# A two-layer decoder trunk on one core: router logits reordered around the last token tiles, a shorter token table, fewer identity products

## What is computed

```python
x = x + g_m * y                      # residual after the mixer's output product
h = modulate(rms_norm(x, norm_ffn[i]), sh_f, sc_f)
# hier_moe(h):
g_prob = softmax(t @ w_group);  g_idx = argmax(g_prob + b_group)
e_logit = (t @ w_router)[..group g_idx..];  e_prob = softmax(e_logit)
_, e_idx = top_k(e_prob + b_router[g_idx], 2)      # two experts of 32 for each token
out[token] += weight * (silu(t @ w1[e]) * (t @ w3[e])) @ w2[e]
```

## Time and profile before

| | us |
|---|---|
| median of 3 runs | 1144.45 |
| lowest and highest | 1142.14, 1145.19 |
| the profiled execution | 1145.37 |
| its span in the trace | 1143.6 |

### The profile page before, as it was taken

How to read it: one execution, slowest core, us unless ns; L and a number is a source line. 1 busy time by engine, 2 the same in 40 slices (tenths; PEclk the granted TensorE clock), 3 DMA queues, 4 the chain that set the end, 5 groups by cost and what they waited for, 6 DMA issues and landing times.

```text
span 1143.6 us, 15372 instructions
## 1 busy us (share of the span) xinstructions
PE 1049.5 (92%) x5698; PEld 637.9 (56%) x5698; DVE 608.2 (53%) x1464; ACT 328.1 (29%) x894; POOL 91.9 (8%) x129
## 2 busy tenths in 40 slices
PE   4999999999998999897889999999999999978997
PEld 3444444655466666564556566655457765655663
DVE  6899988897646322221256577767235622212224
ACT  4321122874231111111124545666112112111110
POOL 1000000000011111111000000000000111101110
PEclk9999999999998999999999999999998999999999
DMA  9929868918468999999996200301826799999999
GB/s 368 402 76 404 330 255 336 421 56 354 167 269 350 401 418 418 418 418 419 416 386 265 111 1 28 146 13 38 337 94 267 298 412 421 419 411 406 419 416 360
DMA packets 66816, 341.45 MB, mean 299 GB/s; under 512 B 11111, under 2 KB 11367, under 8 KB 36401
## 3 DMA queue, kind: packets, MB, share of 16 engines
q1 hardware_dynamic: 49952, 297.68, 64.5%
q0 software_dynamic: 15120, 37.63, 8.5%
q10 hardware_dynamic: 1664, 5.09, 1.1%
HBM read 320.90 MB, written 37.24 MB: 313 GB/s over the span
## 4 chain that ended last, share of the span: by engine, by line
PE 79%; DMA 7%; DVE 5%; issue 3%; ACT 3%; SPq 2%; DVEq 0%; ACTq 0%; POOLq 0%
PE PP L888 18%; PE PP L681 12%; PE PP L796 10%; PE PP L903 9%; PE PP L703 3%; DMA AHS<-in_moe_w 3%; PE PP L1111 3%; PE PP L1071 3%; PE PP L654 2%; PE PP L861 2%; PE PP L1115 2%; PE PP L740 2%; PE PP L751 2%; PE PP L690 2%; SPq L518 2%
## 5 line engine op out<-in xcount | busy, mean ns | idle before, releaser
L681 PE MATMUL PP<-ring,AHS 128*128 128x512 f32 x320 | 139.9, 592 | 0.0
L1982 DVE TENSOR_TENSOR PS<-PS,PP 128x256 f32<-128x256 f32 x33 | 13.9, 421 | 195.7 <-PE PP L888 186.1
L796 PE MATMUL PP<-ring,AHS 128*128 128x512 f32 x256 | 111.3, 593 | 1.4 <-ACT AHS L1444 0.8
L1989 DVE SCALAR_TENSOR_TENSOR PS<-PP,small,GF 128x512 f32<-128x512 f32 x66 | 46.5, 746 | 110.2 <-PE PP L903 100.3
L681 PEld LDWEIGHTS PP<-ring,AHS 128*128 128x128 f32 x320 | 59.7, 190 | 69.8 <-issue 69.8
L888 PE MATMUL PP<-RQK,RV 128*64 128x256 f32 x640 | 75.4, 392 | 10.1 <-issue 8.0
L796 PEld LDWEIGHTS PP<-ring,AHS 128*128 128x128 f32 x256 | 48.1, 190 | 59.7 <-issue 59.7
L888 PE MATMUL PP<-ring,RV 128*64 128x256 f32 (+1 forms) x608 | 75.6, 389 | 6.2 <-issue 3.2
L1502 ACT ACTIVATE PS<-PP 128x256 f32<-128x256 f32 x33 | 12.7, 384 | 216.6 <-PE PP L888 216.6
L888 PEld LDWEIGHTS PP<-RQK,RV 128*64 128x64 f32 x640 | 56.1, 142 | 32.0 <-issue 18.6
L888 PE MATMUL PP<-AHS,RV 128*64 128x256 f32 x640 | 71.7, 379 | 0.3 <-issue 0.3
(11 more groups left out here) (348 smaller groups left out, 1677.7 us busy)
## 6 DMA issues: line engine op xcount, KB each, us to landing
AHS<-in_moe_w SPq DMA_DIRECT2D x61, 1024.0 KB, 22.6
ring<-in_moe_w SPq DMA_DIRECT2D x58, 1024.0 KB, 19.6
RQK<-in_moe_w SPq DMA_DIRECT2D x52, 1024.0 KB, 20.2
ring<-in_ada_t SPq DMA_DIRECT2D x22, 1024.0 KB, 8.4
AHS<-in_ada_t SPq DMA_DIRECT2D x18, 1024.0 KB, 7.5
X<-in_moe_w SPq DMA_DIRECT2D x16, 1024.0 KB, 22.3
ring<-in_da_w_qkv SPq DMA_DIRECT2D x10, 1024.0 KB, 11.1
RQK<-in_ada_t SPq DMA_DIRECT2D x8, 1024.0 KB, 6.6
```

What stands on the lines that cost most here:

```text
L681: last = mm(PB[qkv_bank(n)][:, :], HT[:, c, t * P:(t + 1) * P], us[c // 4][:, (c % 4) * NH:(c % 4 + 1) * NH], start=c == 0, stop=c == C - 1)
L796: last = mm(PB[2 * t + n][:, :], (OT, OTM)[l][:, k, t * P:(t + 1) * P], us[k // 2][:, (k % 2) * D + n * NH:(k % 2) * D + (n + 1) * NH], st ...
L1989: last = stt(ysb[b][:, cols], PB[5 + m][:, :], weight, GF[:, cols], ALU.mult, ALU.mult)
```

## The change

1. In `project_out`, the seven identity products are gone and the logits of tile 2 stand in their place, ahead of turning tile 3. Tile 2 adds its chunks in the order 4 to 7, 0 to 3; tile 3 in the order 0, 1, 4, 5, 2, 3, 6, 7.
2. `logits` waits before every second chunk for the engine that writes it, no longer for the whole tile from both engines. For the fourth tile in the norms k = 1 and 3 each engine signals twice, after its first two chunks and after its last two. Two helper functions compute the counts.
3. `norm` on ScalarE modulates chunk 0 of tile 2 ahead of the squares of tile 3, and chunks 1 to 3 behind them. `norm` on VectorE modulates tile 2 ahead of normalising tile 3.
4. `token_v` holds S - token for both experts, and `idx` is written by one instruction in the place of three.
5. The last `keep_busy` in `route` has 16 products in layer 1, and still 22 in layer 0.

The places it touches, as a diff:

```diff
+def by_scalar(k, t, half=1):
+    last = k % 2 and t == T - 1
+    return 4 * k + k // 2 + t + 1 + (half if last else 0)
+
+def by_vector(k, t, half=1):
+    return by_scalar(k, t, half) - T
 ...
                 def logits(t):
-                    modulated(k1, t)
-                    for c in range(C):
+                    order = {2: (4, 5, 6, 7, 0, 1, 2, 3), 3: (0, 1, 4, 5, 2, 3, 6, 7)}.get(t, range(C))
+                    for n, c in enumerate(order):
+                        if c % 2 == 0:
+                            name, count = (("hA", by_scalar), ("hD", by_vector))[c // 4]
+                            pe.wait_ge(sem(name), count(k1, t, c // 2 % 2))
 ...
                 transpose_x(k1, 2)
                 logits(1)
-                keep_busy(3, 7)
+                logits(2)
                 transpose_x(k1, 3)
-                logits(2)
                 logits(3)
 ...
-                keep_busy(3, 22)
+                keep_busy(3, 16 if l else 22)
 ...
             def norm(k):                                   # ScalarE
                 squares(k, 0)
-                for t in range(T):
-                    if t + 1 < T:
-                        squares(k, t + 1)
-                    modulate(k, t)
+                squares(k, 1)
+                modulate(k, 0)
+                squares(k, 2)
+                modulate(k, 1)
+                modulate(k, 2, (0,))
+                squares(k, 3)
+                modulate(k, 2, (1, 2, 3))
+                modulate(k, 3)
 ...
             def norm(k, update):                           # VectorE
                 for t in range(T):
                     update((k - 1) // 2, t)
+                    if t == T - 1:
+                        modulate(k, t - 1)
                     normalise_x(k, t)
-                    if t:
+                    if 0 < t < T - 1:
                         modulate(k, t - 1)
 ...
-                ts(second[:, 0:PAIRS], PB[2][:, 0:PAIRS], S + 0.5, -float(S), ALU.is_le, ALU.mult)
-                link(ts(empty[:, 0:PAIRS], PB[2][:, 0:PAIRS], -1.0, 2.0 * S, ALU.mult, ALU.add))
-                tt(idx[:, 0:PAIRS], empty[:, 0:PAIRS], second[:, 0:PAIRS], ALU.add).then_inc(sem("idx"), 1)
+                ts(idx[:, 0:PAIRS], PB[2][:, 0:PAIRS], -1.0, float(S), ALU.mult, ALU.add).then_inc(sem("idx"), 1)
```

More of the change, by code:

```diff
@@ L628, in modulated @@
             def modulated(k, t):
-                pe.wait_ge(sem("hA"), 4 * k + t + 1)
-                pe.wait_ge(sem("hD"), 4 * (k - 1) + t + 1)
+                pe.wait_ge(sem("hA"), by_scalar(k, t))
+                pe.wait_ge(sem("hD"), by_vector(k, t))
             def turn_x(t, chunks):
@@ L801, in logits @@
                 def logits(t):
-                    modulated(k1, t)
-                    for c in range(C):
+                    order = {2: (4, 5, 6, 7, 0, 1, 2, 3), 3: (0, 1, 4, 5, 2, 3, 6, 7)}.get(t, range(C))
[3 more added lines that the diff above has]
+                            pe.wait_ge(sem(name), count(k1, t, c // 2 % 2))
                         last = mm(PB[0][:, t * NR:(t + 1) * NR], HT[:, c, t * P:(t + 1) * P], WGR[:, c, :],
-                                  start=c == 0, stop=c == C - 1)
+                                  start=n == 0, stop=n == C - 1)
                     last.then_inc(sem("lg"), 1)
@@ L1208, in squares, with modulate @@
                 fn(sd[:, t:t + 1], ss[:, t:t + 1], ACT.Sqrt, bias=eps, scale=1.0 / D).then_inc(sem("sd"), 1)
-            def modulate(k, t):
+            def modulate(k, t, chunks=range(C // 2)):
                 l, w = divmod(k, 2)
@@ L1214, in modulate @@
                 act.wait_ge(sem("xt"), 4 * k + t)
-                for c in range(C // 2):
+                for c in chunks:
                     last = fn(HT[:, c, t * P:(t + 1) * P], PB[2 * t][:, c * P:(c + 1) * P], ACT.Identity,
                               bias=MODC[:, l, 3 * w + V_SHIFT, c:c + 1], scale=GC[:, k, c:c + 1])
-                last.then_inc(sem("hA"), 1)
+                    if c == C // 2 - 1 or w and t == T - 1 and c == 1:
+                        last.then_inc(sem("hA"), 1)
             def norm(k):
                 squares(k, 0)
-                for t in range(T):
-                    if t + 1 < T:
-                        squares(k, t + 1)
-                    modulate(k, t)
+                squares(k, 1)
[6 more added lines that the diff above has]
+                modulate(k, 3)
             def root(out_, in_, scale, s):
@@ L1674, in modulate @@
                               MODC[:, l, 3 * w + V_SHIFT, c:c + 1], ALU.mult, ALU.add)
-                last.then_inc(sem("hD"), 1)
+                    if c == C - 1 or w and t == T - 1 and c == C // 2 + 1:
+                        last.then_inc(sem("hD"), 1)
             def norm(k, update):
@@ L2301, in tables @@
                     g.iota(steps1, [[1, NPAIR]], base=1, channel_multiplier=0, allow_small_or_imprecise_dtypes=True)
-                    g.iota(token_v, [[-P, T], [-S, 2]], base=2 * S, channel_multiplier=-1, allow_small_or_imprecise_dtypes=True)
+                    g.iota(token_v, [[-P, T], [0, 2]], base=S, channel_multiplier=-1, allow_small_or_imprecise_dtypes=True)
                     g.iota(token1, [[P, T], [S, 2]], base=1, channel_multiplier=1,
```

## The result

| | before | after |
|---|---|---|
| median, 12 executions each | 1142.12 | 1144.1 |
| lowest and highest | 1140.91, 1145.19 | 1142.45, 1147.1 |
| span of the profiled execution | 1143.6 | 1144.5 |

The ratio is 1.0021 with a 95% interval of 1.0011 to 1.0031: slower by some 2.4 us (the two medians are 2.0 apart). That is under the 0.3% that the prediction named as its bound of "the same", and inside the stated range, but on the other side of the old time than forecast. The changed kernel again (e17), in another set of 12 executions, gave 1.0016 (1.0003 to 1.0029). Both profiled executions took longer than the median of their kernels, by 3.3 and 2.2 us (1145.37 and 1146.27).

A forecast was written before the change was run, and what follows sets the result against it. TensorE's chain through filler bound layer 1, the gather's transfer layer 0. Layer 0 gave 0, layer 1 -0.4 + 0.28 + 1.1 = 1.0 gained: span 1143.6 to 1142.6, plus 1.77, less 0.92, is 1143.5; range 1140.7 to 1146.3.

The forecast's parts named there:

- VectorE's four chunks: Layer 1: tile 2's modulation ends at 869.1, before tile 3's reciprocal at 869.33, with 0.2 to spare.
- Rival A: The clock holds through the logits; layer 1 gains 3.1, layer 0 1.4, giving 1140.0; chance 0.15.
- part 1: Layer 1, tile 2's logits ahead of tile 3's turn: earlier clock fall, at 871.2, logits end 877.2 against 876.80, 0.4 lost.
- case of a 1.8 loss: Layer 1: the clock falls at 869, tile 2's ScalarE half is slow too, logits end at 878.6.
- rival B: Low clock reaches into tile 2's second half, tile 3's turn late in both layers; 0.6 or 2.2 slower; chance 0.14.
- The 16 identities behind el run as before; I charge nothing there: Layer 1, identity products behind the logits: still 5.64 at mixed levels, the clock's return unchanged, cost nothing.
- Part 2: Layer 0, same new order: 0.4 lost, bounds 1.5 gained and 1.5 lost; with the idx gain about 0 left.
- Part 3: Routing in each layer: idx written by one instruction gains 0.28 on the path.
- Part 4: Layer 1, 16 identities instead of 22 behind idx: 1.37 off the start of the gathered rows' turn, 1.1 kept.
- the branch for which I had written 0.2: Layer 1's shorter cover with the clock at 2.4 GHz throughout: the gather's landing is late next, gain only 0.2.
- rival C: The shorter cover gains nothing since DMA carries layer 1's experts; 1.0 gained becomes -0.1, giving 1144.5; chance 0.15.
- The rule weighed in part 1: Transpose-mode matmuls don't count as busy for the clock gate as others do; fall at the early end, logits end 878.6.

The follow-up runs named there:

- e17: The changed kernel measured again in another set of 12 executions; ratio 1.0016 to the kernel before.
- e3: The kernel before with 16 instead of 22 identity products at the end of layer 1's routing, nothing else; ratio 0.9999 to the kernel before.
- e15: The changed kernel with TensorE's old order, seven identity products included, back in layer 1, so the new order is in layer 0 alone; ratio 0.9995 to the kernel before.
- e6: The changed kernel with 22 instead of 16 identity products behind idx in layer 1; ratio 1.0026 to the kernel before.
- e7: The changed kernel with four identity products between the turn of tile 3 and its logits; ratio 1.0011 to the kernel before.
- e14: The kernel before with SyncE's two weight transfers in layer 1 issued without waiting for the second gather; ratio 1.0018 to the kernel before.

## Why the prediction was right or wrong

**The time came out near the forecast by luck.** 1144.1 is 0.6 over the forecast 1143.5, but the forecast was 0.95 faster than a median of 1144.45 that three executions gave; over twelve the kernel before has 1142.12. The forecast gain was a loss of 2.0 to 2.4.

**The reading of the stretch held.** The clock does fall in the run of narrow products, earlier than before, in both layers, and the turn of tile 3 does start behind tile 2's logits. VectorE's four chunks fitted (866.52 to 867.89, the reciprocal at 868.03). Rival A, in which the clock holds, was not seen in any profile of the new order without the identities.

**The step that failed is the size of part 1: the "loss of 0.4" in layer 1.** Measured against the output product, the logits ended 12.1 - 10.5 = 1.6 later in layer 1 and 1.8 later in layer 0. I put the fall at 871.2; it came at 869.36, which is 870.6 in the old kernel's terms, when the ScalarE half of tile 2's logits had just begun (869.10). That half took 1.7 where I had 0.85, so the turn of tile 3 began 0.6 later than forecast. The turn itself took 1.95 where I had 1.6, near the upper bound and not the middle, and 0.2 more came behind it. My case of a 1.8 loss stood at a fall at 869, and rival B's at one before 870.3; nearly that loss came with a later fall, so I had put the fall too late, and had also priced a given fall too low.

**A second step failed beside it: "The 16 identities behind el run as before; I charge nothing there".** An earlier fall did not bring an earlier return. The low level lasted twice as long, those products took 6.20 instead of 5.64, and the ranks were made 2.1 later (+19.0 for +16.9). I had charged the logits only up to their own end. Together the two steps make 2.1 lost at the ranks of layer 1 where 0.4 was forecast, and that is what the end shows: +279.5 for +277.3.

**And the reference point was a poor one.** The kernel before doesn't always lose what its one profile showed: in layer 1 of e3, which is untouched up to the ranks, the low stretch was 3.4 us and the ranks stood at +15.8. The prediction took the one profile's 1.1 us of slow logits as what the change would be measured against, while the same code has executions in which the clock loss is smaller; the order without identities had a stretch of 10 to 14 us in every profile. That widens the loss of the mean beyond that of the pair of profiles.

**Part 2, layer 0:** loss in the stretch 1.8, which is beyond the bound of 1.5 that I gave; what is left of it at the second gather is 0.7, and e15 shows nothing at the end. "About 0" was right, through the transfers, as argued, and from layer 0's last output product to layer 1's the changed kernel took no longer (536.2 for 536.5).

**Part 3:** 0.28 gained before the cover in each layer, seen (0.55 to 0.27).

**Part 4:** the cover shortened as computed, but no gain of it was resolved at the end (e3 0.9999). I kept 1.1. In the changed kernel the gather landed 1.33 behind the cover's end, and in e6 all 22 products ended with the landing, so the six were hardly on the path: the level was high throughout the cover, which is the branch for which I had written 0.2. This is rival C's price by another mechanism than the one I gave it: by the account that fits, the transfers count as the later of two.

**Rival B** was the nearest: the low clock reaching back into tile 2's second half. It gave 1.8 and 1.5 lost; seen 1.6 and 1.8. Its total of 0.6 slower is a wrong sum: 1.8 + 1.5 - 0.56 - 1.1 is 1.6, which is nearer to what was measured, though it still has the filler's 1.1 and nothing for the ranks. The rule weighed in part 1 (the Trainium skill, "TensorE: Matmul & The Clock Gate", Part 4: PE-mode transpose) put the fall at the early end, 869, against 871.2 as my middle. It came at 870.6 in those terms, between the two, which neither proves nor refutes the rule; no kernel here ran the turns alone.

## What to carry to other kernels

Filler on an otherwise idle engine can be load-bearing for the work behind it: before replacing identity products by real but narrow work, look at what the granted clock did behind them, and take them out alone once (here 1.0052). One profile doesn't stand for its kernel: look at the granted clock of all executions, as e7 shows. When the clock's level decides a term, charge it up to the point where the level comes back, and don't measure against a single profile of a kernel whose low stretches vary from one execution to the next. And where two streams meet, as weights and gathers here, ask for each layer apart which one is late: the same 2 us at the ranks left no trace at the end of layer 0 and cost their full price in layer 1.

## What the runs showed of the hardware

- The clock can fall with TensorE busy. In layer 1 of the changed kernel TensorE was 100, 67, 100 and 93% busy in the four microseconds from 866 to 870, and the clock went to 1.2 GHz at 869.36; the work was 128x40 products and turns. In all 14 layers profiled without the seven 128x128 identity products (1.8 us of work) it fell 4.1 to 5.5 us after the last output product; in the 22 with them not before +8.4, and in seven of these not before the ranks.
- Levels change what the products cost in this proportion: eight logit products 1.88 and 3.63, the eight turns 1.04 to 1.10 and 1.95.
- Stretches at 1.2 GHz of 3.4, 6.8, 10.2 and 13.6 us occur, and the same code shows different ones in different executions.
- An indirect gather of 128 rows landed after 4.2 us on quiet queues, 4.4 from issue to the turn that waits for it in both layers of the changed kernel, 7.1 when two 1 MB transfers had been put ahead of it (e14), and 10.2 among the experts' weights.
